# Laying the buffers that TensorE loads as stationary lowest in the partition, in a two-layer encoder step

## What is computed

```python
def swiglu_ffn(x, w_gate, w_up, w_down):            # 1024 -> 4096 -> 1024
    return (jax.nn.silu(x @ w_gate) * (x @ w_up)) @ w_down
...
for i in range(DEPTH):                               # DEPTH = 2
    x = x + 0.5 * rms_norm(swiglu_ffn(rms_norm(x, pre[i, 0]), ...), post[i, 0])
    x = x + rms_norm(mixer(rms_norm(x, pre[i, 1])), post[i, 1])   # GLA, then SGU
    x = x + 0.5 * rms_norm(swiglu_ffn(rms_norm(x, pre[i, 2]), ...), post[i, 2])
```

## Time and profile before

| | |
|---|---|
| median of 3 runs | 2141.49 us (2140.75 to 2141.72) |
| profiled execution, its own time | 2141.62 us |
| span of that execution, first to last instruction | 2139.5 us |
| TensorE matmuls (PE) busy | 2126.2 us, 99% of the span, 11108 records |
| weight loads (PEld) busy | 1926.1 us, 90% |
| DVE, ACT, POOL busy | 844.9 us, 722.7 us, 276.9 us (39%, 34%, 13%) |
| mean granted TensorE clock | 0.998 of full |
| chain that ended last | 98% on PE |

### The profile page before, as it was taken

One profiled execution on the slowest core, in us unless ns is written; L12 is line 12 of the kernel. 1 busy time (PEld: TensorE's weight loads), 2 busy tenths in 40 slices (PEclk: granted clock), 3 DMA queues, 4 the chain that ended last, 5 costly groups with the idle time before them and its releaser, 6 DMA issues.

```text
span 2139.5 us, 25773 instructions
## 1 busy us (share of the span) xinstructions
PE 2126.2 (99%) x11108; PEld 1926.1 (90%) x11108; DVE 844.9 (39%) x814; ACT 722.7 (34%) x831; POOL 276.9 (13%) x275
## 2 busy tenths in 40 slices
PE   9999999999999999999999999999999999999998
PEld 6999999888789999998899999988988889999997
DVE  4423233436563233325423233355744453332333
ACT  4322323443343233224322323243333343222331
POOL 1000000001200000000000000020444400000000
PEclk9999999999999999999999999999999999999999
DMA  5443334343435333442443334334444334343331
GB/s 195 158 132 124 119 118 138 126 152 132 155 119 176 119 118 121 135 134 91 150 152 123 119 119 137 127 130 163 159 132 133 133 105 162 119 137 118 119 123 65
DMA packets 187203, 282.76 MB, mean 132 GB/s; under 512 B 6850, under 2 KB 144322, under 8 KB 186964
## 3 DMA queue, kind: packets, MB, share of 16 engines
q1 hardware_dynamic: 182930, 267.39, 38.4%
q0 software_dynamic: 4016, 13.67, 2.0%
q10 hardware_dynamic: 146, 0.07, 0.0%
HBM read 273.24 MB, written 7.86 MB: 131 GB/s over the span
## 4 chain that ended last, share of the span: by engine, by line
PE 98%; issue 0%; POOL 0%; ACT 0%; DVE 0%; DMA 0%; DVEq 0%; POOLq 0%; ACTq 0%
PE bank L1240 17%; PE bank L1239 17%; PE bank L1241 17%; PE bank L1249 10%; PE bank L1251 10%; PE bank L1250 10%; PE bank L1219 4%; PE bank L1221 4%; PE bank L1220 4%; PE bank L1500 1%; PE bank L1206 1%; PE bank L1375 1%; PE bank L1376 1%; PE bank L1377 1%; PE bank L1411 0%
## 5 line engine op out<-in xcount | busy, mean ns | idle before, releaser
L701 DVE TENSOR_TENSOR wlo_sb<-raw_sb,whi_sb 128x2048 fp32r<-128x2048 f32 x242 | 553.8, 2291 | 857.5 <-ACT whi_sb L422 857.5
L1239 PE MATMUL bank<-xhi_sb,whi_sb 128*128 128x384 f32 x2048 | 686.5, 335 | 0.0
L1240 PE MATMUL bank<-xlo_sb,whi_sb 128*128 128x384 f32 x2048 | 685.7, 335 | 0.0
L1241 PE MATMUL bank<-xhi_sb,wlo_sb 128*128 128x384 f32 x2048 | 685.4, 335 | 0.0
L422 ACT ACTIVATE whi_sb<-raw_sb 128x2048 fp32r<-128x2048 f32 x242 | 461.0, 1909 | 343.8 <-PE bank L1251 336.7
L1239 PEld LDWEIGHTS bank<-xhi_sb,whi_sb 128*128 128x128 f32 x2048 | 385.0, 188 | 3.6 <-issue 0.8
L1240 PEld LDWEIGHTS bank<-xlo_sb,whi_sb 128*128 128x128 f32 x2048 | 385.2, 188 | 2.9
L1241 PEld LDWEIGHTS bank<-xhi_sb,wlo_sb 128*128 128x128 f32 x2048 | 385.1, 188 | 0.0
L1251 PE MATMUL bank<-whi_sb,hlo_sb 128*128 128x512 f32 x768 | 303.6, 395 | 0.0
L1249 PE MATMUL bank<-whi_sb,hhi_sb 128*128 128x512 f32 x768 | 303.5, 395 | 0.0
L1250 PE MATMUL bank<-wlo_sb,hhi_sb 128*128 128x512 f32 x768 | 302.9, 394 | 0.0
(11 more groups left out here) (156 smaller groups left out, 1383.8 us busy)
## 6 DMA issues: line engine op xcount, KB each, us to landing
raw_sb<-ffn_w_up SPq DMA_DIRECT2D x64, 1024.0 KB, 5.4
raw_sb<-ffn_w_down SPq DMA_DIRECT2D x64, 1024.0 KB, 4.9
raw_sb<-ffn_w_gate SPq DMA_DIRECT2D x62, 1024.0 KB, 5.4
raw_sb<-sgu_w_in SPq DMA_DIRECT2D x24, 1024.0 KB, 5.2
raw_sb<-gla_w_in SPq DMA_DIRECT2D x12, 1024.0 KB, 5.2
raw_sb<-sgu_w_out SPq DMA_DIRECT2D x12, 1024.0 KB, 4.8
gla_state_sample<-s_sb POOLq DMA_DIRECT2D x4, 1024.0 KB, 4.9
raw_sb<-gla_w_out SPq DMA_DIRECT2D x4, 1024.0 KB, 6.8
```

Of the source, the lines that this page charges most:

```text
L701: dve.tensor_tensor(wlo[:, n % NSLOT], raw[:, n % NRAW], whi[:, n % NSLOT].bitcast(F32), ALU.subtract)\
L1239: pe.matmul(out, w_hi_part, xhi[:, k, :], start=k == 0, stop=False)
L1240: pe.matmul(out, w_hi_part, xlo[:, k, :], start=False, stop=False)
L1241: mm = pe.matmul(out, w_lo_part, xhi[:, k, :], start=False, stop=k == DK - 1)
```

## The change

The declarations are put in another order. `hhi`, `hlo`, `ohi`, `olo`, `uhi`, `ulo`, `qk` and `v_rows`, which were in the shared part at the top of the partition, get a shared part of their own right above the constants (with `w_rows`, `mixed` and `b_spatial`, which fit in there). Above it come `xhi`, `xlo`, `whi` and `wlo`; the residual `x`, the raw weights, the norms' gains and the small statistics follow; the rest of the shared part ends where it ended.

```diff
-        x = sb("x", [P, NT, D])
+
+        hhi, hlo = shared(("hhi", [P, 8, TOK], F32R), ("hlo", [P, 8, TOK], F32R))
+        v_rows, qk = shared(("v_rows", [P, HEADS, NT, DV], F32), ("qk", [P, HEADS, 2, TOK], F32))
+        olo, ohi = shared(("olo", [P, HEADS * VT, TOK], F32R), ("ohi", [P, HEADS * VT, TOK], F32R))
+        uhi, ulo, mixed, b_spatial = shared(
+            ("uhi", [P, 6, TOK], F32R), ("ulo", [P, 6, TOK], F32R), ("mixed", [P, 2, TOK], F32),
+            ("b_spatial", [P, SPATIAL, P], F32))
+        (w_rows,) = shared(("w_rows", [P, 2, SPATIAL, P], F32))
+        sb("stationary_of_stage", [P, 2 * 8 * TOK])
         xhi = sb("xhi", [P, DK, TOK], F32R)
         xlo = sb("xlo", [P, DK, TOK], F32R)
-        raw = sb("raw", [P, NRAW, CHUNK])
         whi = sb("whi", [P, NSLOT, CHUNK], F32R)
         wlo = sb("wlo", [P, NSLOT, CHUNK], F32R)
+        x = sb("x", [P, NT, D])
+        raw = sb("raw", [P, NRAW, CHUNK])
...
-        z, hhi, hlo, silu_g, h_up, rows_g = shared(
-            ("z", [P, 2, D], F32), ("hhi", [P, 8, TOK], F32R), ("hlo", [P, 8, TOK], F32R),
-            ("silu_g", [P, 2, TOK], F32), ("h_up", [P, 2, TOK], F32), ("rows_g", [P, NT, BANK], F32))
+        z, silu_g, h_up, rows_g = shared(
+            ("z", [P, 2, D], F32), ("silu_g", [P, 2, TOK], F32), ("h_up", [P, 2, TOK], F32), ("rows_g", [P, NT, BANK], F32))
```

More of the change, by code:

```diff
@@ L119, in build_trunk @@
         sb("to_line_stage", [P, 24])
-        z, hhi, hlo, silu_g, h_up, rows_g = shared(
-            ("z", [P, 2, D], F32), ("hhi", [P, 8, TOK], F32R), ("hlo", [P, 8, TOK], F32R),
-            ("silu_g", [P, 2, TOK], F32), ("h_up", [P, 2, TOK], F32), ("rows_g", [P, NT, BANK], F32))
-        (_, wz, wz_hi, wz_lo, w_gate2, z_cols, v_rows, qk, k_dec, log_g, e_neg, e_pos, s0) = shared(
+        z, silu_g, h_up, rows_g = shared(
+            ("z", [P, 2, D], F32), ("silu_g", [P, 2, TOK], F32), ("h_up", [P, 2, TOK], F32), ("rows_g", [P, NT, BANK], F32))
+        (_, wz, wz_hi, wz_lo, w_gate2, z_cols, k_dec, log_g, e_neg, e_pos, s0) = shared(
             ("under_z", [P, 2, D], F32), ("wz", [P, DK, RANK], F32), ("wz_hi", [P, DK, RANK], F32R),
             ("wz_lo", [P, DK, RANK], F32R), ("w_gate2", [RANK + 1, BANK], F32), ("z_cols", [32, TOK], F32),
-            ("v_rows", [P, HEADS, NT, DV], F32), ("qk", [P, HEADS, 2, TOK], F32), ("k_dec", [P, HEADS, TOK], F32),
+            ("k_dec", [P, HEADS, TOK], F32),
             ("log_g", [P, HEADS * TOK], F32), ("e_neg", [P, HEADS, TOK], F32), ("e_pos", [P, HEADS, TOK], F32),
@@ L132, in build_trunk @@
         b_cum = log_g[:, :].rearrange("p (h t) -> p h t", h=HEADS)
-        (scores, k_rows, og, v_pair, q_pair, s_prompt, olo, ohi, _, r_silu) = shared(
+        (scores, k_rows, og, v_pair, q_pair, s_prompt, _, r_silu) = shared(
             ("scores", [P, TOK], F32), ("k_rows", [P, TOK], F32), ("og", [P, NT, DV], F32),
             ("v_pair", [P, 2, DV], F32), ("q_pair", [P, 2, P], F32), ("s_prompt", [P, NCH, DV], F32),
-            ("olo", [P, HEADS * VT, TOK], F32R), ("ohi", [P, HEADS * VT, TOK], F32R),
             ("under_k_dec", [P, HEADS, TOK], F32), ("r_silu", [P, NT, D], F32))
[L139 to L142, removed]
+        (_, v, ln_rows, w_turned, ln_stats, ln_mean_var, ln_var, ln_rstd) = shared(
+            ("under_z2", [P, 2, D], F32), ("v", [P, NT, HALF], F32), ("ln_rows", [P, 2, 2, WIDE], F32),
+            ("w_turned", [P, 2, SPATIAL, P], F32),
             ("ln_stats", [P, NT, VB, 6], F32), ("ln_mean_var", [P, NT, 2], F32), ("ln_var", [P, NT], F32),
             ("ln_rstd", [P, NT], F32))
-        (u_act, _, _, w_rows) = shared(
-            ("u_act", [P, 4, TOK], F32), ("rest_of_z", [P, 2 * D - 4 * TOK], F32), ("under_v", [P, NT, HALF], F32),
-            ("w_rows", [P, 2, SPATIAL, P], F32))
+        (u_act,) = shared(("u_act", [P, 4, TOK], F32))
         banks = [ctx.enter_context(nc.psum_tensor(f"bank{i}", [P, BANK], F32)) for i in range(8)]
```

## The result

The changed kernel takes 2130.91 us (median of five executions, 2129.98 to 2130.94 but for one) against 2141.49: a ratio of 0.9949, interval 0.9937 to 0.9961. One execution of the changed kernel took 5455 us; it was disturbed and is left out of the ratio, and without it the median is 2130.63. The change gains 10.6 us (10.9 by the median of the other four); the forecast was 16.5.

A forecast was written before the change was run, and what follows sets the result against it. TensorE's back-to-back matmuls were taken as the bound, time being number by spacing. Savings of 12.9, 2.8 and 0.8 us sum to 16.5: 2141.6 to 2125 us, own range 2122 to 2130, 8 in 10 from 2121 to 2137.

The forecast's parts named there:

- the first rival: Height of the stationary tile in the partition is the cause: 16.5 us gained in down, 2125 us; chance 0.72.
- the second: Height is only part of the 5.6 ns in down: half the gain, 2133.4 us; chance 0.11.
- The third: The loop form of down, changing bank after three matmuls, is the cause and place does nothing: 2141.6 us; chance 0.12.
- The fourth: Nearness of the two operands costs, so 6144 cols_tile matmuls could pay 5.6 ns each: 34.4 us, 2159.5 us; chance 0.04.
- the floor: In down, no row showed fewer than 13 ns beyond the columns, so 226.7 ns a matmul was taken as lowest.
- Feed-forward, forecast 12.9 us: Feed-forward down: 2304 matmuls going from 232.3 to 226.7 ns save 12.9 us.
- SGU, forecast 2.8: down in SGU: 432 matmuls going from 233.2 to 226.7 ns save 2.8 us.
- GLA, forecast 0.8: down in GLA: 144 matmuls going from 232.4 to 226.7 ns save 0.8 us.
- `cols_tile`, forecast 0: Moving xhi, xlo, whi, wlo costs 0; cols_tile should keep 173.3 ns.
- if `down` settled between: Sign of a wrong size: down spacing ending between 226.7 and 232 ns, instead of 36 matmuls spanning 7.93 us.

The follow-up runs named there:

- experiment 2: Changed kernel with whi and wlo moved to the top of the partition (163,584 to 229,120), activations still lowest: 2163.11 us, ratio 1.01.
- experiment 9: Changed kernel with 128 bytes more padding between the activations, still lowest, and xhi, xlo, whi, wlo: 2140.96 us, ratio 1.0.
- experiment 3: Changed kernel with the stationary activations above the weights, at 110,976 to 135,552, instead of below xhi: 2130.05 us, ratio 0.9947.
- experiment 8: Kernel before the change with 128 bytes more padding ahead of the shared part, activations staying high at 158,592 to 213,888: 2130.31 us, ratio 0.9948.
- experiment 7: TensorE-only probe, encoder step left out, stationary tile moved against streaming rows by 32-byte steps: 512 columns took 226.4 ns at 0 apart, 228.9 to 234.3 otherwise.

## Why the prediction was right, and where it was wrong

**What bounds the kernel: right.** TensorE's spacing was what moved, and most of its saving reached the end. One reading was too coarse: the clock is not "granted in full (2.4 GHz) in all slices". A slice of the page is 53 us long, and within one the granted clock fell to its lower level, 1.2 GHz, for 3.4 us, just behind GLA's gate matmuls of 17 rows; in the profile after the change 3.4 us at that level come at the start of the kernel instead, behind the waits for the first `wlo` (stretch, us, PE busy, clock, DMA share, GB/s, before and after):

```profile
466.57:469.97 3.40, 3.40 (x12) 0.50 0.22 71
...
19.09:22.49 3.40, 3.40 (x12) 0.50 0.90 276
```

In the first, 384 columns take 320 ns instead of 173, which makes about 1.6 us; the start of the kernel takes as much longer after the change, so the two cancel here. The profiles of experiments 2 and 9 show no such fall from 15 to 2130 us, that of experiment 3 shows both. A difference of 1 or 2 us between two executions need not be one of spacing.

**The cause: wrong.** The step that failed is "All stationary tiles that pay 13 lie below byte 139,648, all that pay 19 and more above 158,464". The sentence is true of the rows, but the same rows divide in the same way by the start modulo 256: 0 for the three activation buffers, 128 for all that streams past them. Height and offset went together in the kernel before, and I looked at one. Experiments 8 and 9 separate them: high at the same offset 2130.3 us, low at another 2141.0. That the time came out between 2121 and 2137 us is luck as far as the cause goes: the move happened to bring the activations to the weights' offset, and moving down by itself is worth nothing (experiment 9). The cause was in none of the four rivals; 0.01 had been left for what was not thought of. Nor was the number near: 2130.9 lies past the first rival's own range of 2122 to 2130, and nearer to the second's 2133.4 than to its 2125.

**The other rivals.** The third, that the form of `down` costs and the place does nothing, is refuted by experiment 8, where the form is untouched; it was right that height does nothing. The fourth looked at the pair of operands, which is where the cause lies, but at their nearness, and saw a loss in it; `cols_tile` kept its pace. (The two gaps that it called equally wide are 18,816 and 16,384 bytes; nothing hung on that.) The Trainium skill, "SBUF — State Buffer", section "Who interferes with whom", gives TensorE two independent read ports and names no dependence on place. Experiment 7 differs: 226.7 ns against 232.4 with all other engines idle, by the offset of the two reads alone. The measurement decides here.

**The size: the floor was mis-sized.** "I take 226.7 as the floor" holds for a stream that has come to rest, not for a call. The opening of a call adds about 41 ns (its nine steps add up to 2,082 ns instead of 9 x 226.7 = 2,040), so 36 matmuls span 7.97 us and not 7.93. By terms:

- Feed-forward, forecast 12.9 us: 52 calls of 36 by 8.13 - 7.97 = 0.16, and four tails of 0.53 to 0.57: 8.3 + 2.2 = 10.5. The step from a call to the gate and up tiles behind it also fell, from 236 to 227 ns: 0.5.
- SGU, forecast 2.8: 7.93 - 7.72 = 0.21 for 36 of 432 matmuls, 2.5. GLA, forecast 0.8: 7.90 - 7.72 = 0.18 for 36 of 144, 0.7.
- `cols_tile`, forecast 0: its 96 matmuls behind a call take 16.49 us and not 16.47, so 0.02 us is given back in each of 52 places, 1.1. Its opening after a call reads 171 175 177 185 176 182 now; in experiment 9, behind a call that is out of step, it reads 171 179 174 173.

10.5 + 0.5 + 2.5 + 0.7 - 1.1 = 13.1 us, against 12.9 of the span. Of these the median shows 10.6; the rest was lost outside the sum. The profiled execution takes 3.4 us beyond its span, where the kernel before took 2.1; that is 1.3. The median of the changed kernel lies 0.9 above its profiled execution, that of the kernel before 0.1 below. The time beyond the span is as uneven in experiment 8 (2.1 to 3.5 us) and steady in experiment 9 (2.1 to 2.4), so in these runs it goes with the faster pace. What it is stays open; no run was made for it.

**What would show it.** The prediction would be wrong in size "if `down` settled between": the mean of a call did, at 227.8, though the stream comes to rest at the floor. `rows_group`, `cols_tile` (but for its opening) and the waits stayed as foretold.

## What to carry to other kernels

When two matmuls of one shape show two spacings, list the start of each operand modulo 256 before looking at anything larger. With float32r (the rounded type of `hi` and `lo`) and 384 or 512 columns, give the stationary tile and the rows that stream past it the same start modulo 256; where tiles begin at multiples of 256 bytes in their buffers, as here, one pad does it. At 256 columns it was not the faster choice (below). Where two properties divide the rows alike, as place and offset did here, the rows don't choose between them: the cheapest kernel that holds one and moves the other does, and here it was one number in the source.

## What the runs showed that I had not expected

- The offset between the stationary and the streaming operand sets the pace of float32r matmuls with period 256 bytes. For 512 columns 0 bytes apart gives 226.7 ns; with the tile 192 above the rows it is 229.0, and every other step of 32 gives 232.4 to 234.3. Even 4 bytes give 232.4, and 8 bytes 230.6. Why is not shown.
- It depends on width and type. 384 columns keep 173.3 to 173.4 ns with the tile 0, 32, 96 or 192 bytes above, and take 174.6 to 176.7 at the rest. 256 columns take 120.0 at 0 and 118.6 at 128. bfloat16 with 512 columns takes 215.8 at all four offsets tried. Beyond the 213.3 ns of its 512 columns float32r pays 13.4 at best and bfloat16 2.5. The Trainium skill, "TensorE: Matmul & The Clock Gate", section "Back-to-back issue gap", gives columns / 2.4 + 2.5 ns as the gap of an isolated matmul in a warm array, and about 131 ns as the sustained spacing of 512 columns, without a word on the type. The bfloat16 blocks, which run back to back, take what the first figure gives; the float32r blocks take more, and no block here comes near 131 ns.
- A change of width has a price of its own, about 40 ns over nine matmuls. In experiment 7, behind matmuls of 384 columns whose operands were both at 0 modulo 256, blocks with both at 64 had none (226.7 from the first step), those with both at 128 a shorter one (five steps). It wasn't tried whether an offset of `x` could spare the trunk its openings: 52 calls at 41 ns are 2.1 us.
